# q1's heads turned on VectorE in four pieces, in a two-layer hybrid decoder trunk

## The reference

```
q, k, v, q_mem = split(h @ w_in)             # 12 heads of 128 for q, k, v; 4 for q_mem
q = rmsnorm_per_head(q) * q_g                # over the 128 of a head
k = rmsnorm_per_head(k) * k_g
z = q @ k.T * 128 ** -0.5
w = exp(log_sigmoid(z) + later_log_1m)       # sums of log_sigmoid(-z) over keys between
o = w @ v                                    # causal
p = softmax(rmsnorm(q_mem) @ k_mem.T * 128 ** -0.5);  o_mem = p @ v_mem
x = x + concat(o, o_mem) @ w_out
```

## Time and profile before

| | |
|---|---|
| median of 3 runs | 794.86 us (794.66 to 794.86) |
| profiled execution | 795.67 us, span 793.9 us |
| TensorE busy | 788.5 us, 99% |
| VectorE busy | 626.7 us, 79% |
| ScalarE busy | 434.1 us, 55% |
| GpSimd busy | 66.0 us, 8% |
| chain that ended last | TensorE 99% of it |

### The profile page before, as it was taken

The page is one execution under the profiler, slowest core; times in us unless marked ns, Lnnn a source line. Parts: engine busy times, 40 slices in busy tenths (PEclk is TensorE's granted clock), DMA queues, the critical chain, the costliest instruction groups (busy, mean ns, idle before and its releaser), DMA issues.

```text
span 793.9 us, 9669 instructions
## 1 busy us (share of the span) xinstructions
PE 788.5 (99%) x3712; PEld 655.5 (83%) x3712; DVE 626.7 (79%) x936; ACT 434.1 (55%) x520; POOL 66.0 (8%) x94
## 2 busy tenths in 40 slices
PE   8999999999999999999999999999999999999998
PEld 5988888888888888888888888888888888888886
DVE  4688989887758788888988877788776678888862
ACT  4677774566436454444346586676563735445430
POOL 4010023320000000000000000133230000000000
PEclk9999999999999999999999999999999999999999
DMA  7754556543546656655645555444345566665551
GB/s 247 284 170 159 160 199 220 175 149 110 174 151 202 210 180 194 205 178 200 205 166 197 175 159 163 160 155 140 125 159 158 171 201 195 183 206 195 178 210 53
DMA packets 85453, 141.38 MB, mean 178 GB/s; under 512 B 3438, under 2 KB 50960, under 8 KB 85408
## 3 DMA queue, kind: packets, MB, share of 16 engines
q1 hardware_dynamic: 84416, 139.73, 53.8%
q10 hardware_dynamic: 608, 0.93, 0.3%
q0 software_dynamic: 384, 0.11, 0.1%
HBM read 139.68 MB, written 1.07 MB: 177 GB/s over the span
## 4 chain that ended last, share of the span: by engine, by line
PE 99%; DMA 1%; SPq 0%; DVE 0%; issue 0%; DVEq 0%
PE acc L1418 29%; PE acc L1420 29%; PE acc L1419 29%; PE bank L1415 3%; PE bank L1540 1%; PE acc L1643 1%; PE bank L1568 1%; PE bank L1588 1%; DMA raw<-in_ssd_w_in 1%; PE bank L1616 1%; PE bank L1594 1%; PE bank L1606 1%; PE bank L1595 0%; PE bank L1617 0%; PE bank L1550 0%; PE bank L1546 0%
## 5 line engine op out<-in xcount | busy, mean ns | idle before, releaser
L1037 DVE TENSOR_TENSOR lo<-raw,hi 128x2048 fp32r<-128x2048 f32 (+2 forms) x129 | 291.9, 2266 | 60.1 <-ACT hi L704 58.9
L704 ACT ACTIVATE hi<-raw 128x2048 fp32r<-128x2048 f32 (+2 forms) x129 | 241.6, 1879 | 86.0 <-DMA raw<-in_ffn_w_gate_up 43.6
L1418 PE MATMUL acc<-lo,aT_hi 128*128 128x512 f32 (+1 forms) x660 | 257.4, 390 | 0.0
L1420 PE MATMUL acc<-hi,aT_lo 128*128 128x512 f32 (+1 forms) x660 | 253.9, 385 | 0.0
L1419 PE MATMUL acc<-hi,aT_hi 128*128 128x512 f32 (+1 forms) x660 | 253.6, 384 | 0.0
L1420 PEld LDWEIGHTS acc<-hi,aT_lo 128*128 128x128 f32 x660 | 123.9, 188 | 25.1
L1418 PEld LDWEIGHTS acc<-lo,aT_hi 128*128 128x128 f32 x660 | 124.0, 188 | 24.2 <-issue 0.2
L1419 PEld LDWEIGHTS acc<-hi,aT_hi 128*128 128x128 f32 x660 | 124.0, 188 | 24.0 <-issue 0.2
L1267 DVE STREAM_TRANSPOSE uT<-un 32x256 f32<-32x256 f32 (+1 forms) x192 | 79.4, 414 | 3.1
L1418 PE MATMUL acc<-lo,uT_hi 128*128 128x512 f32 x176 | 68.6, 390 | 0.0
L1420 PE MATMUL acc<-hi,uT_lo 128*128 128x512 f32 x176 | 68.5, 389 | 0.0
(11 more groups left out here) (219 smaller groups left out, 867.0 us busy)
## 6 DMA issues: line engine op xcount, KB each, us to landing
raw<-in_ffn_w_gate_up SPq DMA_DIRECT2D x88, 512.0 KB, 4.8
raw<-in_ffn_w_down SPq DMA_DIRECT2D x22, 1024.0 KB, 4.8
raw<-in_sb_w_in SPq DMA_DIRECT2D x20, 1024.0 KB, 5.1
raw<-in_ssd_w_in SPq DMA_DIRECT2D x14, 1024.0 KB, 5.1
raw<-in_mem_w_kv SPq DMA_DIRECT2D x8, 1024.0 KB, 5.0
raw<-in_ssd_w_out SPq DMA_DIRECT2D x8, 1024.0 KB, 4.9
raw<-in_sb_w_out SPq DMA_DIRECT2D x8, 1024.0 KB, 4.8
seg<-cs_rows SPq DMA_DIRECT2D x6, 384.0 KB, 4.9
```

The source lines that it names most:

```text
L704: return nc.scalar.activation(out_, in_, func, **k)
L1037: v.tensor_tensor(lo[w % RING][:, c], raw[w % RING][:, c], hi[w % RING][:, c].bitcast(F), ALU.subtract).then_inc(lo_ready, 1)
L1418: mm(ps, stat_hi, mov_lo, start=first, stop=False)
L1420: return mm(ps, stat_lo, mov_hi, start=False, stop=last)
```

## The change

q1 is no longer turned by TensorE. Four steps qq, of four 32x256 transposes each, turn the normed block on VectorE into qT, one in unit 82, one in 83 and two in 84; a step qg in unit 85 has ScalarE multiply all of q1 in place by its gain, and z(4) to z(7) wait for that. The eight pq move: pair 0 from units 82 to 85 to units 85 to 88, pair 1 from 89 to 92 to 90, 91 and twice 92. mo of pair 0 moves from unit 86 to unit 90. q2 joins SEEDED: its sum of squares stays in unit 86, its seed and scale are in unit 87, among the MIDDLE steps. With q1's two hT steps gone, the banks of the steps behind them are others, and z(2), z(3), C(0) and C(1) follow q0's transposes in the round.

```diff
@@ -89,7 +89,7 @@
 GC = [(g, c) for g in range(GROUPS) for c in range(TOK)]
 
 
-SEEDED = ["k1", "k2", "q0", "q1"]
+SEEDED = ["k1", "k2", "q0", "q1", "q2"]
 HEAD_NORMS = ["qm0", "km0", "km1", "qm1", "k0", "k1", "k2", "q0", "q1", "q2"]
 
 
@@ -197,17 +197,22 @@
             at(u + 2 * i, ("sps", b), ("C", b - 1), ("C", b))
             at(u + 2 * i + 1, ("O", b - 1), ("O", b))
     for n in ("qm1", "k0", "k1", "k2", "q0", "q1", "q2"):
-        at(block_end(n) + (4 if n == "q2" else 2), ("hT", n, 0), ("hT", n, 1))
+        if n != "q1":
+            at(block_end(n) + (4 if n == "q2" else 2), ("hT", n, 0), ("hT", n, 1))
+    k = block_end("q1") + 2
+    for b, u in enumerate((k, k + 1, k + 2, k + 2)):
+        at(u, ("qq", b))
+    at(k + 3, ("qg",))
     k = block_end("qm1") + 4
     memory_attention(1, (k, k + 2, k + 2, k + 4),
-                     (k + 8, k + 9, k + 10, k + 11, k + 15, k + 16, k + 17, k + 18), (k + 12, k + 19))
+                     (k + 11, k + 12, k + 13, k + 14, k + 16, k + 17, k + 18, k + 18), (k + 16, k + 19))
     for n in HEAD_NORMS[1:-1]:
         if n != "km1":
             at(block_end(n) + 1, ("hn", n))
-        if n in SEEDED:
+        if n in SEEDED[:-1]:
             at(block_end(n) + 1, ("hw", n))
     at(block_end("q2") + 2, ("hr", "q2"))
-    at(block_end("q2") + 3, ("hm", "q2"))
+    at(block_end("q2") + 3, ("hw", "q2"))
     input_transposes(U_FFN1 - 1, 3)
 
 
@@ -215,14 +220,16 @@
 
 
 
-NO_BANK = ("hw", "pq", "ksq", "kq", "kg", "gate", "silu", "seg", "segm", "pn", "dt", "memsq", "memnorm", "sps", "zd", "hn", "hr", "hm", "tq", "ts")
-
-EARLY, MIDDLE = ("seg", "pn", "zd", "sps", "hn"), ("segm", "hw")
+NO_BANK = ("qq", "qg", "hw", "pq", "ksq", "kq", "kg", "gate", "silu", "seg", "segm", "pn", "dt", "memsq", "memnorm", "sps", "zd", "hn", "hr", "hm", "tq", "ts")
+
+EARLY, MIDDLE = ("seg", "pn", "zd", "sps", "hn"), ("segm", "hw", "qg")
 USES = {s: i for i, s in enumerate(s for u in sorted(PLAN) for s in PLAN[u] if s[0] not in NO_BANK)}
 
 NAT = {"B": ("xb", 0, 1), "qm0": ("hT", "qm0", 1), "C": ("xb", 1, 1), "xs0": ("xb", 2, 1),
        "xs1": ("xb", 3, 1), "xs2": ("xb", 4, 1), "km0": ("hT", "km0", 1), "km1": None}
-NAT.update({n: ("hT", n, 1) for n in ("qm1", "k0", "k1", "k2", "q0", "q1", "q2")})
+NAT.update({n: ("hT", n, 1) for n in ("qm1", "k0", "k1", "k2", "q0", "q2")})
+NAT["q1"] = None
+NAT["q2"] = NAT.pop("q2")
 NAT_ORDER = list(NAT)
 assert HEAD_NORMS == [n for n in NAT_ORDER if n[0] in "kq"]
 CONV_TILES = [12, 16, 0, 4, 8]
@@ -878,6 +885,10 @@
                 elif kind == "Bn":
                     wait_full(act, step)
                     read(step, f(bn[:].rearrange("p g n -> p (g n)"), T(step)[:]))
+                elif kind == "qg":
+                    act.wait_ge(S("queries_turned"), 4)
+                    q_ = qT[:, 4:8, :].rearrange("p h t -> p (h t)")
+                    f(q_, q_, scale=gq_scaled).then_inc(S("queries_gained"), 1)
                 elif kind == "hw":
                     act.wait_ge(S("head_mean"), SEEDED.index(step[1]) + 1)
                     link(f(hl8, hv8, ACT.Ln))
@@ -1301,6 +1312,16 @@
                 elif kind == "hn":
                     head_rstd(step[1])
                     head_scale(step[1])
+                elif kind == "qq":
+                    b = step[1]
+                    if b == 0:
+                        dve.wait_ge(S("nat_normed"), HEAD_NORMS.index("q1") + 1)
+                    rows = natb("q1")[:].rearrange("p t (h n) -> p t h n", n=P)
+                    cols_ = qT[:, 4:8, :].rearrange("p h (t n) -> p t h n", n=P)
+                    for a in range(4):
+                        last = v.transpose(cols_[32 * b:32 * b + 32, :, :, 32 * a:32 * a + 32],
+                                           rows[32 * a:32 * a + 32, :, :, 32 * b:32 * b + 32])
+                    last.then_inc(S("queries_turned"), 1)
                 elif kind == "kq":
                     b = step[1]
                     if b == 0:
@@ -1311,6 +1332,8 @@
                         last = v.transpose(cols_[32 * b:32 * b + 32, :, :, 32 * a:32 * a + 32],
                                            rows[32 * a:32 * a + 32, :, :, 32 * b:32 * b + 32])
                     last.then_inc(S("keys_turned"), 1)
+                elif kind == "hr" and step[1] in SEEDED:
+                    head_mean(step[1])
                 elif kind == "hr":
                     head_rstd(step[1])
                 elif kind == "hm":
@@ -1589,8 +1612,11 @@
                                       start=(m == 0), stop=(m == 1))
                 elif kind == "z":
                     h = step[1]
-                    for n in ("k", "q"):
-                        wait_read(pe, ("hT", f"{n}{h // 4}", h % 4 // 2))
+                    wait_read(pe, ("hT", f"k{h // 4}", h % 4 // 2))
+                    if h // 4 == 1:
+                        pe.wait_ge(S("queries_gained"), 1)
+                    else:
+                        wait_read(pe, ("hT", f"q{h // 4}", h % 4 // 2))
                     mm(b[:, 0:SEQ], kT[:, h, 0:P], qT[:, h, :], start=True, stop=True)
                     last = mm(b[:, SEQ:SEQ + P], kT[:, h, P:SEQ], qT[:, h, P:SEQ], start=True, stop=True)
                 elif kind == "C":
```

## The result

The changed kernel takes 798.3 us (median of 6 runs, 797.88 to 799.12) against 794.68 (6 runs, 794.56 to 794.86): the ratio is 1.0042, interval 1.0032 to 1.0052. It is 3.6 us slower.

The account below looks back on a forecast made before the run. TensorE, which never waits in units 82 to 95, was taken as the bound. -0.88 + 1.6 + 0 + 1.7 + 1.1 = +3.5 us on 794.86 gave 798.4 us, own range 797.7 to 799.2, 8-in-10 range 796.7 to 799.8.

Parts of the forecast that it names:

- Part 1: q1's eight transposes leave TensorE, which saves their whole price there, 0.88 us.
- Part 2: Unit 84: two transpose pieces on VectorE, then ScalarE's gain multiply, make score product z(4) wait 1.6 us.
- Part 3: Units 86 to 90: q2's shorter norm and the moved memory product add nothing; C(4) waits 0.2 us at most.
- Part 4: Unit 88: zd(6) and zd(7) read their PSUM banks later, so value products O(4) and O(5) wait 1.7 us.
- Part 5: Two softmax pieces in unit 92 make sp_lo late, so C(10) in unit 93 waits 1.1 us.
- just pays: Unit 86: q2's norm chain of 13 small operations becoming one makes up for the added softmax piece of 1.82 us.
- only the first wait: Rival: after z(4)'s wait the whole pipeline has shifted and later waits vanish, 795.6 us; chance 0.07.
- All of it hidden: Rival: z(4)'s gain is ready by its turn and the change gives its 0.88, 794.0 us; chance 0.06.
- one wait absent: Rival: one of the three waits of TensorE does not occur, 796.7 to 797.3 us; chance 0.11.
- GpSimd held up: Rival: VectorE's transposes lock out GpSimd's masks, in one or two of four places, 800 to 802 us; chance 0.10.

Follow-up runs that it names:

- e5: The kernel before the change, with each of q1's eight TensorE transposes issued twice: 795.84 us, ratio 1.0012.
- e1: Changed kernel with q1's second piece in unit 82 and third in 83, leaving one in unit 84: 797.08 us, ratio 1.0026.
- e4: Changed kernel with q1's pieces in units 82, 82, 83, 84, pair 0 in 85, 86, 88, 89, pair 1 in 90, 90, 91, 92: 794.62 us, ratio 0.9994.
- e8: e4 with q1's pieces in units 81, 82, 82, 83 instead of 82, 82, 83, 84: 794.74 us, ratio 0.9997.
- e9: e8 with ScalarE's multiply of q1 in unit 84 instead of 85: 794.29 us, ratio 0.9991.
- e7: Changed kernel with q2's old norm of 13 linked small operations in unit 86 and its scale behind C's corrections: 800.89 us, ratio 1.0081.
- e2: Changed kernel with pair 0's third and fourth softmax pieces in units 88 and 89 instead of 87 and 88: 797.61 us, ratio 1.0034.
- e10: e9 with q1's pieces in units 82, 82, 83, 83 instead of 81, 82, 82, 83: 795.48 us, ratio 1.0006.
- e3: Changed kernel with pair 1's softmax pieces in units 90, 90, 91, 92 instead of 90, 91 and two in 92: 797.75 us, ratio 1.0032.
- e6: Changed kernel with q2's small operations and scale behind C(4) and C(5)'s corrections on VectorE in unit 87: 798.28 us, ratio 1.0047.

## Why the prediction was right

Forecast were 798.4 us; measured are 798.3. By its parts:

**Part 1, -0.88.** C(0) stands 13.46 us behind z(0) instead of 14.36: -0.90. e5 shows the same price with the other sign, 0.86.

**Part 2, +1.6 before z(4).** 1.73, and as named: eight transposes, multiply, z. The 0.1 more is the step from the multiply's end, 527.82, to z(4): 0.14, where I had put 0.05. e1 takes the wait away and leaves 0.2. I said there that ScalarE is idle by the time the transposes end. That holds in the changed kernel, where it was idle for 1.4 us ahead of the multiply. But e4, e8 and e9 show that with the pieces placed earlier the multiply behind the conversion of unit 85 ends too late by itself, so that VectorE alone could not give all of it back.

**Part 3, nothing.** C(4) did not wait. The memory product's move is neutral: C(4) is 1.7 nearer to C(2) and C(8) 1.7 farther from C(6). e7 shows that "just pays" was right within half a microsecond, with more room than I gave it.

**Part 4, +1.7 before O(4) and O(5).** The mechanism is as forecast: the time of O(4) is the end of zd(6), O(5)'s that of zd(7), shown by the rows above, by e2 and by e10. The size is the term that was off: 0.81 + 0.40 and 0.09 of restart, 1.3 in the profiled execution. I had started VectorE's sum at 539.89, a time that contains a weight correction of 2.91 us, slowed by GpSimd. In the changed kernel it took 2.29. In e3, where the same code met GpSimd the other way, the wait was 1.7. One reading in this part was wrong, though the sum doesn't use it: by the earlier trace rows the bank was free 1.6 before O(4) and 1.2 before O(5), not 1.2 and 0.5.

**Part 5, +1.1 before C(10).** 1.23, and e3 takes it away with nothing in its place.

Of the rivals, "only the first wait" falls with e1 and e3, since the waits are independent. "All of it hidden" and "one wait absent" did not happen. "GpSimd held up" by transposes is excluded by the rows of e6. The rule that a 128x128 transpose belongs on TensorE (the Trainium skill, VectorE: DVE Perf Modes, Rules for kernel authors) was borne out for the changed kernel by 3.6 us, and by e9, with 16 transposes on VectorE and 0.66 us less, it was not: what decided was where they stood.

The error of the size in part 4 was 0.4, those of parts 2 and 5 are 0.1 each the other way, and some 0.2 lie in restarts behind the waits, of under 0.1 each; so it is luck that the sum came out nearer than its parts. The low ends of the four terms add up to 797.4, not to the 797.7 given as the forecast's own range; the measured time lies in both.

## What to carry to other kernels

Where TensorE never waits, price a move onto another engine by unit: list for each of TensorE's steps how early its inputs are ready (before the change 0.7 us at C(10), 1.2 at O(5), 1.6 at O(4)), and set each added instruction against the first step behind it. Count PSUM banks and buffers as inputs too, since a late last reader of one stops a step that has no data from it. And place added pieces by the room of each gap: the same 16 transposes and eight softmax pieces cost 3.6 us as first placed, and gained 0.7 in e9. There two pieces of q1 still share unit 82, but the gap has room for all but 0.15 us of them.

## What the runs showed that I had not expected

How long a weight correction takes on VectorE depends on how it meets a GpSimd mask. In unit 86 of the changed kernel, VectorE and GpSimd:

```profile
536.03 2.29 DVE L1048 TENSOR_TENSOR lo<-raw,hi 128x2048 fp32r<-128x2048 f32 x1 [0.84 <-ACT hi L711]
```

```profile
535.36 3.56 POOL L677 TENSOR_TENSOR spb<-spb,tlt 128x256 f32<-128x256 f32 x2
```

and the same place in e3:

```profile
536.21 2.90 DVE L1048 TENSOR_TENSOR lo<-raw,hi 128x2048 fp32r<-128x2048 f32 x1 [0.84 <-ACT hi L711]
```

```profile
535.53 1.43 POOL L677 TENSOR_TENSOR spb<-spb,tlt 128x256 f32<-128x256 f32 x2
```

Two masks alone take 1.43 us. After, the correction has its 2.29, and the pair of masks takes 3.56, as if the second were held until the correction is over. In e3 the masks have their 1.43, and the correction takes 2.90, as if it were held. That the one which comes first goes on and the other is held is my reading of these durations, and not shown: the second mask starts at 536.06 in the one and at 536.22 in the other, within 0.03 us behind the correction's recorded start in both. The same pair meets in unit 84, where it makes the wait before z(4) 1.7 (correction 2.29: changed kernel, e3) or 2.0 (correction 2.91: e2, e6, e7), in code that is the same up to there. So 0.3 to 0.5 us of such a wait hang on a meeting that a prediction from one trace cannot foresee. By the Trainium skill (GPSIMD Engine Reference, Specifications) the two engines contend when a VectorE instruction has two SBUF inputs. The correction has, and the trace agrees by these rows; the transposes, with one input, are free of it by e6's.
